# Sparse-attention stage of a fused two-block kernel: heads taken in pairs on parts of the TensorE array, instead of one head at a time

## The reference

```python
pc = softmax(where(mc, q @ kc.T * scale, NEG_2))      # compressed: 31 keys
o_c = pc @ vc
ps = softmax(causal(q @ ks.T * scale)); o_s = ps @ vs  # selected
pw = softmax(causal(q @ kw.T * scale)); o_w = pw @ vw  # window
y_nsa = g[..., 0:1] * o_c + g[..., 1:2] * o_s + g[..., 2:3] * o_w
mixed = concatenate([y_nsa * silu(z_nsa), y_lru * silu(z_lru), y_conv * silu(z_conv)])
x = x + mixed @ w_out
```

## Time and profile before

| | us |
|---|---|
| median of 3 runs | 2950.22 |
| profiled execution, its own time | 2948.79 |
| its span | 2947.0 |
| TensorE matmul busy | 2793.0 (95%) |
| TensorE weight load busy | 2185.3 (74%) |
| VectorE busy | 1504.0 (51%) |
| ScalarE busy | 1149.8 (39%) |
| GpSimd busy | 1059.3 (36%) |

### The profile page before, as it was taken

One profiled execution on the slowest core, in us unless ns is written; L12 is line 12 of the kernel. 1 busy time (PEld: TensorE's weight loads), 2 busy tenths in 40 slices (PEclk: granted clock), 3 DMA queues, 4 the chain that ended last, 5 costly groups with the idle time before them and its releaser, 6 DMA issues. The chain is left out here.

```text
span 2947.0 us, 37005 instructions
## 1 busy us (share of the span) xinstructions
PE 2793.0 (95%) x12850; PEld 2185.3 (74%) x12860; DVE 1504.0 (51%) x2736; ACT 1149.8 (39%) x1915; POOL 1059.3 (36%) x430
## 2 busy tenths in 40 slices
PE   7999999999999899898999999998999898999898
PEld 6857776678888688576666788885887776887676
DVE  2067544572323310875364633325788565788564
ACT  2234434252323333344342432324247443247443
POOL 4422112334444334121123444442347411347411
PEclk9999999999999999999999999999999999999999
DMA  4211111222232223111112322321223101224101
GB/s 157 92 58 51 43 36 44 86 79 93 94 106 86 86 79 99 36 53 41 36 53 76 100 95 90 104 95 57 86 93 129 44 29 51 86 93 133 40 32 49
DMA packets 60888, 220.28 MB, mean 75 GB/s; under 512 B 6880, under 2 KB 7008, under 8 KB 60640
## 3 DMA queue, kind: packets, MB, share of 16 engines
q1 hardware_dynamic: 60192, 217.12, 22.1%
q10 hardware_dynamic: 576, 1.57, 0.2%
HBM read 216.57 MB, written 2.10 MB: 74 GB/s over the span
## 5 line engine op out<-in xcount | busy, mean ns | idle before, releaser
L428 POOL TENSOR_TENSOR w_lo<-w_raw,w_hi 128x1024 fp32r<-128x1024 f32 x404 | 1009.2, 2508 | 1855.4 <-ACT w_hi L411 1842.5
L402 PE MATMUL bank<-x_hi,w_hi 128*128 128x512 f32 x2128 | 895.1, 421 | 47.4 <-DVE x_lo L2323 17.0
L404 PE MATMUL bank<-x_hi,w_lo 128*128 128x512 f32 x2128 | 838.2, 394 | 0.0
L403 PE MATMUL bank<-x_lo,w_hi 128*128 128x512 f32 x2128 | 837.4, 394 | 0.0
L411 ACT ACTIVATE w_hi<-w_raw 128x1024 fp32r<-128x1024 f32 x400 | 418.6, 1053 | 469.4 <-PE bank L404 457.9
L402 PEld LDWEIGHTS bank<-x_hi,w_hi 128*128 128x128 f32 x2128 | 406.0, 191 | 166.3 <-issue 56.2
L404 PEld LDWEIGHTS bank<-x_hi,w_lo 128*128 128x128 f32 x2128 | 404.3, 190 | 87.7
L403 PEld LDWEIGHTS bank<-x_lo,w_hi 128*128 128x128 f32 x2128 | 406.5, 191 | 83.1 <-issue 12.7
L402 PE MATMUL bank<-rhs_hi,w_hi 128*128 128x512 f32 (+1 forms) x656 | 262.3, 400 | 4.0 <-DVE rhs_lo L1427 4.0
L403 PE MATMUL bank<-rhs_lo,w_hi 128*128 128x512 f32 (+1 forms) x656 | 255.6, 390 | 0.0
L404 PE MATMUL bank<-rhs_hi,w_lo 128*128 128x512 f32 (+1 forms) x656 | 255.3, 389 | 0.0
(11 more groups left out here) (405 smaller groups left out, 3629.0 us busy)
## 6 DMA issues: line engine op xcount, KB each, us to landing
w_raw<-w SPq DMA_DIRECT2D x404, 512.0 KB, 3.4
ln_in<-x SPq DMA_DIRECT2D x1, 2048.0 KB, 7.9
out<-residual SPq DMA_DIRECT2D x8, 256.0 KB, 2.2
p_raw<-p ACTq DMA_DIRECT2D x2, 512.0 KB, 3.9
constants<-con SPq DMA_DIRECT2D x1, 455.0 KB, 3.3
cos<-cos SPq DMA_DIRECT2D x1, 256.0 KB, 3.5
sin<-sin SPq DMA_DIRECT2D x1, 256.0 KB, 3.7
params_b<-prm_b ACTq DMA_DIRECT2D x1, 256.0 KB, 2.6
```

Of the source, the lines that this page charges most:

```text
L402: nc.tensor.matmul(out, wh, xh, start=first, stop=False)
L403: nc.tensor.matmul(out, wh, xl, start=False, stop=False)
L404: S.last = nc.tensor.matmul(out, wl, xh, start=False, stop=last)
L428: S.nc.gpsimd.tensor_tensor(S.wl[s][:, :], S.raw[s][:, :], S.wh[s][:, :].bitcast(F32), ALU.subtract).then_inc(S.lo_ready[s], 1)
```

## The change

Eight heads make four pairs: head `t` of group 0 and head `t` of group 1, whose features lie on partitions 0 to 63 and 64 to 127 of the same tile. A pair step is one `t`, one query block and one branch; there are 32 in a layer, and `HeadPair` holds its operands.

- Scores: no padded query tile. Each head's 64 rows are multiplied by the 64 key rows of its group (row parts of the array), one head into `X[0]`, the other into `X[1]`, then a mask matmul for each. There is one bank for each head, so the scores of pair n+1 wait for the exponentials of pair n.
- Probabilities: VectorE forms gate over row sum (`share`), and ScalarE multiplies the probabilities by it in place (`scale`). The scaled probabilities are turned as before; VectorE copies all of them out of PSUM.
- Values: the values are the stationary operand (64 columns) and the turned probabilities the moving one (128 columns). Head 0 writes partitions 0 to 63 and head 1 partitions 64 to 127 of one bank (column parts of the array), feature-major. The compressed branch is one more term of the same sum, and both branches accumulate in the same PSUM columns.
- The token-major sum, its additions, the zeros and query copies, the product of the compressed branch ahead of the stage, and the 16 transposes behind it go. The gating by `silu(z_nsa)` and the split run inside the stage, one feature tile for each `t`.
- The filling tiles stay 64, two in each pair step. Columns of `z_nsa` and rows of `w_out` are permuted in the host's layout of the weights.

```diff
+class HeadPair:
+    def __init__(self, S, n):
+        t, r = divmod(n, 2 * QB)
+        self.t, (self.b, self.branch) = t, divmod(r, 2)
+        self.w = (self.b + 1) * P
+        self.key, self.value = ((S.kv["ks"], S.vtok["s"]), (S.kv["kw"], S.vtok["w"]))[self.branch]
+        self.bank = (S.ps[3], S.X[3])[t % 2]
+        self.probs, self.turned = ((S.wk[4:6], S.wk[6:8]), (S.wk[0:2], S.wk[2:4]))[n % 2]
+NPAIR = 4 * QB * 2
+def nsa_pe(S, pe, L, ident, fill):
+    def scores(n):
+        h = HeadPair(S, n)
+        if n >= 1:
+            pe.wait_ge(Z.p, 2 * (p0 + n))
+        for e in range(2):
+            nc.tensor.matmul(S.X[e][:, 0:h.w], S.q[half(e), h.t * SEQ + h.b * P:h.t * SEQ + h.w], h.key[half(e), 0:h.w],
+                             start=True, stop=False, skip_group_check=True)
+        for e in range(2):
+            nc.tensor.matmul(S.X[e][:, h.b * P:h.w], S.idb[:, :], S.causb[:, :], start=False, stop=True,
+                             skip_group_check=True).then_inc(Z.s, 1)
+    def turn(n):
+        h = HeadPair(S, n)
...
+        for c in Z.ptc:
+            pe.wait_ge(c, p0 + n)
+        for e in range(2):
+            pe.wait_ge(S.nsa_scaled, 2 * (p0 + n) + e + 1)
+            for k in range(h.b + 1):
+                m = nc.tensor.transpose((S.X[2], S.ps[2])[e][:, k * P:(k + 1) * P], h.probs[e][:, k * P:(k + 1) * P], ident)
+            m.then_inc(Z.pt, 1)
+    def values(n):
+        h = HeadPair(S, n)
+        if n % (2 * QB) == 0 and h.t >= 2:
+            pe.wait_ge(S.mn_y, L * 4 + h.t - 1)
+        for c in Z.ptc:
+            pe.wait_ge(c, p0 + n + 1)
+        terms = []
+        if h.branch == 0:
+            c0 = lambda e: (2 * h.b + e) * P
+            terms.append(lambda e: (S.vbd[:, (4 * e + h.t) * HD:(4 * e + h.t + 1) * HD], S.cpt[:, c0(e):c0(e) + P]))
+        for k in range(h.b + 1):
+            terms.append(lambda e, k=k: (h.value[:, k * P + e * HD:k * P + (e + 1) * HD], h.turned[e][:, k * P:(k + 1) * P]))
+        for x, term in enumerate(terms):
+            for e in range(2):
+                v, p = term(e)
+                m = nc.tensor.matmul(h.bank[half(e), h.b * P:h.w], v, p, start=(h.branch == 0 and x == 0),
+                                     stop=(h.branch == 1 and x == len(terms) - 1), skip_group_check=True)
+        m.then_inc(Z.o, 1)
+    scores(0)
+    for n in range(NPAIR):
+        if n + 1 < NPAIR:
+            scores(n + 1)
+        fill(2 * n)
+        turn(n)
+        fill(2 * n + 1)
+        values(n)
+def nsa_act(S, act, L, after):
+    def exps(n):
...
+            nc.scalar.activation(h.probs[e][:, 0:h.w], S.X[e][:, 0:h.w], ACT.Exp, bias=S.nm[x][:, :],
+                                 accum_out=S.rs[x][:, :]).then_inc(Z.p, 1)
+    def scale(n):
...
+            act.wait_ge(S.nsa_share, 2 * (p0 + n) + e + 1)
+            t = h.probs[e][:, 0:h.w]
+            nc.scalar.activation(t, t, ACT.Copy, scale=S.rg[e][:, :]).then_inc(S.nsa_scaled, 1)
+    exps(0)
+    scale(0)
+    for n in range(NPAIR):
+        if n + 1 < NPAIR:
+            exps(n + 1)
+            scale(n + 1)
+        after(n)
+def nsa_dve(S, dve, L, after):
+    def share(n, e):
+        h = HeadPair(S, n)
+        dve.wait_ge(Z.p, 2 * (p0 + n) + e + 1)
+        nc.vector.reciprocal(S.rg[e][:, :], S.rs[2 * (n % 2) + e][:, :])
+        dve.drain()
...
+        m = nc.vector.tensor_scalar(S.rg[e][:, :], S.rg[e][:, :], S.gate[:, c:c + 1], None, ALU.mult)
+        m.then_inc(S.nsa_share, 1)
+    def copy(n, e):
+        h = HeadPair(S, n)
+        dve.wait_ge(Z.pt, 2 * (p0 + n) + e + 1)
...
+        nc.vector.tensor_copy(h.turned[e][:, 0:h.w], (S.X[2], S.ps[2])[e][:, 0:h.w]).then_inc(Z.ptc[e], 1)
+    rowmax(0)
+    for e in range(2):
+        share(0, e)
+    for n in range(NPAIR):
+        if n + 1 < NPAIR:
+            rowmax(n + 1)
+        for e in range(2):
+            if n + 1 < NPAIR:
+                share(n + 1, e)
+            copy(n, e)
+        after(n)
...
-        pe.wait_ge(S.nsa.out, (L + 1) * 64 + 2)
-        for k in range(4):
-            for b in range(QB):
-                mm = nc.tensor.transpose(S.X[k][:, b * P:(b + 1) * P], S.ot2[:, b * 512 + k * P:b * 512 + (k + 1) * P], ident)
-            mm.then_inc(S.bt_ready, 1)
-
+        nsa_pe(S, pe, L, ident, lambda n: out_fill(S, pe, L, n // 32, n % 32))
+
+        pe.wait_ge(S.first_added, L * 8 + 9)
...
+        def mix_hi(k):
+            act.wait_ge(S.mn_y, L * 4 + k + 1)
+            nc.scalar.activation(seq(S.mnh, k), seq(S.zn, k), ACT.Copy).then_inc(S.mn_hi, 1)
+
+        def nsa_after(n):
+            if n and n % 4 == 0:
+                i, j = divmod(n // 4 - 1, 4)
+                used(L, B_OUTL + j, i)
+            if n > 8 and n % 8 == 2:
+                mix_hi(n // 8 - 1)
...
+        def mix(k):
+            dve.wait_ge(S.nsa.o, L * NPAIR + 8 * (k + 1))
+            nc.vector.tensor_tensor(seq(S.zn, k), seq(S.zn, k), (S.ps[3], S.X[3])[k % 2][:, :], ALU.mult).then_inc(S.mn_y, 1)
...
+        def nsa_after(n):
+            if n and n % 2 == 0:
+                i, r = divmod(n // 2 - 1, 8)
+                out_add(S, dve, L, i, *divmod(r, 2))
+            if n > 8 and n % 8 == 1:
+                mix(n // 8 - 1)
+            if n > 8 and n % 8 == 3:
+                mix_lo(n // 8 - 1)
+
+        nsa_dve(S, dve, L, nsa_after)
+        mix(3)
+        out_add(S, dve, L, 1, 3, 1)
+        mix_lo(3)
```

More of the change, by code:

```diff
@@ L320, in plan @@
     S.nsa = SoftmaxSems(sem, "nsa")
+    S.nsa_share, S.nsa_scaled = sem("nsa_share"), sem("nsa_scaled")
     S.fox = SoftmaxSems(sem, "fox")
@@ L1601, in pairs_pe @@
     S.last.then_inc(S.unit_done[s], 1)
[L1604 to L1610, removed]
-            for e in range(2):
-                for b in range(QB):
[L1613 to L1632, removed]
@@ new lines, in nsa_dve, with rowmax @@
+def nsa_dve(S, dve, L, after):
+    nc = S.nc
+    Z, p0 = S.nsa, L * NPAIR
+    def rowmax(n):
+        h = HeadPair(S, n)
+        for e in range(2):
+            dve.wait_ge(Z.s, 2 * (p0 + n) + e + 1)
+            nc.vector.tensor_reduce(S.nm[2 * (n % 2) + e][:, :], S.X[e][:, 0:h.w], AX, ALU.max, negate=True).then_inc(Z.max, 1)
+    def share(n, e):
+        h = HeadPair(S, n)
+        dve.wait_ge(Z.p, 2 * (p0 + n) + e + 1)
+        nc.vector.reciprocal(S.rg[e][:, :], S.rs[2 * (n % 2) + e][:, :])
+        dve.drain()
+        c = h.b * 3 * B_HEADS + e * 12 + h.t * 3 + 1 + h.branch
+        m = nc.vector.tensor_scalar(S.rg[e][:, :], S.rg[e][:, :], S.gate[:, c:c + 1], None, ALU.mult)
+        m.then_inc(S.nsa_share, 1)
+    def copy(n, e):
+        h = HeadPair(S, n)
+        dve.wait_ge(Z.pt, 2 * (p0 + n) + e + 1)
+        if n >= 2:
+            dve.wait_ge(Z.o, p0 + n - 1)
+        nc.vector.tensor_copy(h.turned[e][:, 0:h.w], (S.X[2], S.ps[2])[e][:, 0:h.w]).then_inc(Z.ptc[e], 1)
+    rowmax(0)
+    for e in range(2):
+        share(0, e)
+    for n in range(NPAIR):
+        if n + 1 < NPAIR:
+            rowmax(n + 1)
+        for e in range(2):
+            if n + 1 < NPAIR:
+                share(n + 1, e)
+            copy(n, e)
+        after(n)
@@ L1982, in b_scalar @@
             act.wait_ge(S.cpt_ready, L * 2 + h + 1)
[L1983 to L2002, removed]
+            nc.scalar.activation(S.cpt[:, h * SEQ:(h + 1) * SEQ], S.X[2 + h][:, :], ACT.Copy).then_inc(S.cpt_copied, 1)
+        def mix_hi(k):
[7 more added lines that the diff above has]
+                mix_hi(n // 8 - 1)
         used(L, B_PW2)
@@ L2007, in b_scalar @@
             nc.scalar.activation(seq(S.xh, 4 + t), seq(S.zc, t), ACT.Copy).then_inc(S.mc_hi, 1)
[L2009 to L2015, removed]
+        nsa_act(S, act, L, nsa_after)
+        used(L, B_OUTL + 3, 1)
+        mix_hi(3)
         for j in range(4):
```

59 lines of the change are left out of this document (20 added, 39 removed).

## The result

The change makes the kernel slower by 0.3%: 2956.84 us (median of 7 runs, 2954.49 to 2961.6) against 2948.62 for the kernel before in the same sessions, a ratio of 1.003 with a 95% interval of 1.0019 to 1.0041. The profiled execution took 2956.18 us, its span is 2954.4, 7.4 more than before. The time is inside the forecast's range and 1.8 us from its number. Where the time went agrees less well than that number, and so does the difference between the two kernels: 8.2 us, forecast 4.6.

A forecast was written before the change was run, and what follows sets the result against it. TensorE (95% busy) bounds the kernel before; afterwards a cross-engine loop of 151 us a layer does. With entry and end, +2.3 us a layer, 4.6 in all: 2948.8 becomes 2953.4, plus 1.4 for the median, 2955 us; range 2934 to 3000.

The forecast's parts named there:

- Who sets the pace: Attention stage: TensorE before the change (139 us a layer by sum); afterwards a chain over the engines, 151 us a layer.
- The ring: Pair-step loop: scores, maximum, exponential, share, copy, share, copy, values, none side by side; 4.7 us a step, 151 a layer.
- The hand-over from the copy to TensorE: In each pair step, from VectorE's copy of the turned probabilities to TensorE's values: 0.05 us.
- The clock: Stage start: first one or two pair steps at half TensorE speed, 5.3 us and not 3.5; 3 us more.
- The last pair step: Stage end: the final pair step has no scores ahead and is 0.8 us shorter.
- Side by side: Values: both heads' column parts run together, 0.23 us a term; rival one after the other, 0.46 us, 2999 us, 14%.
- the gap behind them: Behind the values' terms, leaving the narrow-output form: 0.13 us taken, bounds 0 and 0.41.
- The entry: Stage start: less ScalarE work ahead, first exponential at 2311.8 us and not 2318.33, scores(1) at 2312.6.
- The chain ahead: Ahead of the stage: VectorE's two zeroing memsets go, so all that follows comes 1.1 us earlier.
- The end: Behind the stage: it ends at 2465.8 us, last third of `w_out` starts at 2466.1, was 2463.83; +2.3 us a layer.
- the fourth gated tile: Stage end: its gating, rounding and difference take 2.1 us beside nine matmuls of 2.05 us.
- the sum: The forecast's item-by-item addition for stage, entry and end: +2.3 us a layer, +4.6 in all.

The follow-up runs named there:

- experiment 1: Third matmul of each filling tile left out, in both kernels: kernel before 2928.4 us (ratio 0.9939), changed kernel 2957.2 us (1.0029).
- experiment 2: Changed kernel with each reciprocal of the shares done twice, with its drain, on VectorE: 2986.33 us, ratio 1.0136.
- experiment 3: Changed kernel with VectorE's two copies of pair n queued ahead of the shares of pair n+1: 2905.0 us; with each reciprocal also doubled, 2906.37 us.
- experiment 4: Changed kernel with the second head's values left out except its first term in each pair step: 2958.55 us, ratio 1.0035.
- experiment 5: Changed kernel with 13, 24 or 64 do-nothing VectorE instructions behind the first layer's stage: 2954.34, 2953.37 and 2953.31 us.

## Why the prediction came out as it did

**Who sets the pace.** Right, in both kernels: experiment 1.

**The ring.** Right in its parts and its size. For the turn shown above the forecast's items give 1.29 + 0.04 to the maximum, 0.69 + 0.03 to the exponential, 0.78 + 0.05 to the reciprocal, 0.37 twice for the shares, 2 x 0.55 - 0.07 for the copies, 0.05 and 0.85 for the values: 5.55 us. The trace has 5.56. In parts: 1.33, 0.72, 0.81, and the rest within 0.1. The hand-over from the copy to TensorE was under-sized (0.14, not 0.05), which the values made up (0.81, not 0.85) with the smaller gaps of VectorE. From scores(1) to the end of the last values it is 2311.91 to 2464.6, 152.7 us; the forecast's is 151 + 3 - 0.8 = 153.2. The near match of the two totals is made of small misses that cancel. Eight pair steps of one `t` take 38.06 us (scores from 2346.62 to 2384.68), forecast 37.9, which is 152.2 a layer and not 151. The clock cost 1.4 us and not 3: only the first pair step was slow, 4.87 us at a granted clock of 0.50 where the same step later takes 3.45. The last pair step is 1.0 shorter, not 0.8. That each share is on the ring: experiment 2. That it is the order of the queue and not VectorE's load: experiment 3. The Trainium skill's rule (TensorEngine Tiling (Array Packing), section PSUM Bottleneck) warned of the copy. The trace agrees that the copy is the limit (28.7 us of waits), but not that it has to be shared out: VectorE was busy for 56 and 59% of the stage, and the order alone was worth 52 us.

**Side by side.** Right: experiment 4. Three terms take 0.81 us, of which 0.69 are the terms and 0.12 the gap behind them, where 0.13 was taken and 0.41 was the bound.

**The entry.** First exponential at 2311.05 (forecast 2311.8), scores(1) at 2311.91 (2312.6), as the timeline of after has it:

```profile
2311.05 0.37 ACT L1686 ACTIVATE work<-bank,neg_max 128x128 f32<-128x128 f32 x1
2311.91 0.80 PE L1626 MATMUL bank<-b_kw,b_q 64*128 64x128 f32 x4 [5.37 <-ACT work L1686]
```

The chain ahead came 1.57 us earlier and not 1.1; of the other 0.5 I know no cause, and this landmark lay between 2303.46 and 2308.71 us in kernels that have the same program up to there, so the 1.57 itself is no measurement of the zeros.

**The end.** Mis-sized by a term that I took as free, the fourth gated tile:

```profile
2464.50 2.41 POOL L424 TENSOR_TENSOR w_lo<-w_raw,w_hi 128x1024 fp32r<-128x1024 f32 x1 [13.13 <-ACT w_hi L407]
2466.18 1.27 DVE L2350 TENSOR_TENSOR nsa_lo<-silu_z_nsa,nsa_hi 128x512 fp32r<-128x512 f32 x1
2467.51 0.50 PE L398 MATMUL bank<-nsa_hi,w_hi 128*128 128x512 f32 x1 [0.47 <-DVE nsa_lo L2350]
```

The last third of `w_out` starts at 2464.69 (forecast 2466.1), but its fourth tile is 0.6 us late: the difference takes 1.27 us instead of the 0.7 of the sum, because it starts 0.73 us before GpSimd's subtraction ends, the same taking of turns as in the convolution. At the first addition layer 1 has +1.72 us, forecast +2.3.

**What was not in the sum.** That the far part of the program stays as it was. The two stages and their ends together bring about +1.7 us by the landmarks, forecast 4.6. Most of that gap is in the second layer, which costs 1.2 us from the copy to the first addition where layer 1 costs 3.3. There the kernel before lost time to its clock:

```profile
2903.96 0.68 PE L402 MATMUL bank<-nsa_hi,w_hi 128*128 128x512 f32 x1 [1.96 <-DVE nsa_lo L2279]
2904.44 0.63 PE L403 MATMUL bank<-nsa_lo,w_hi 128*128 128x512 f32 x1
```

Behind this wait, the one that the earlier trace rows shows for layer 1, its matmuls ran at a granted clock of 0.50 to 0.52 (1.2 GHz), some 0.63 us each until 2907.6, and the kernel after, which doesn't wait 2 us at that place, ran at 1.00. In layer 1 the kernel before had the same wait and a granted clock of 1.00. The forecast had nothing for this.

The convolution brings 5.7. So 2955 met 2956.84 through an error of -2.9 in one place and 5.7 missing in another, and that the number fits is luck. A third part of the luck is the base: 2955 was built on a profiled execution of 2948.8 and a median 1.4 above it, the median before is 2948.62 with all seven runs, and the difference of 8.2 us is nearly twice the 4.6. With the loop's place repaired the measured difference is 3.3 to 6.2 us over the kernel before (experiment 5), and the forecast's 4.6 lies inside that; how much of the -2.9, which comes from one trace of each kernel, is an error of the forecast, these runs do not show.

## What to carry to other kernels

When a new order of hand-written queues shortens how far engines run ahead, add up one turn of the ring item by item from the old trace before counting what the array saves; and then look for an item that can step out of it by its place in its queue alone: here two lines were worth 52 us, more than the whole array packing gained or lost. Compare the traces also where the diff changes nothing, because a time that fits can be the sum of two misses.

## What the hardware showed that I had not expected

- Every 128 instructions of VectorE's program (2672, 2800 and the like, within two) there is a spot that costs mostly 0.41 to 0.48 us when it is passed with nothing to hide it, and 0.20 to 0.24 us in each pass of a loop of 18 instructions that starts on it (0.77 to 0.81 instead of 0.57 us between passes). Removing 77 small instructions elsewhere put the loop there; 13, 24 or 64 more took it off, and 128 more put it on the next spot.
- A VectorE addition of 128x512 with both operands in SBUF, 0.69 us alone, waits until GpSimd's running subtraction is over: 4.54 us for two of them, and 1.27 for a subtraction that began 0.73 us before GpSimd's end.
- Two heads' scores on row parts cost what one costs (1.13 us for 512 columns); two heads' values on column parts 0.81 us for three terms and as much with the second head left out of two of them.
